# One layer of a streaming encoder with a mixture of experts: the last expert block's rows added into the results by transfers that add

## The chip, the cores and the metric

One Trainium2 chip, one of its cores. The metric is the device time of one execution in microseconds (us), the median of several runs. The core has TensorE (PE; PEld is its weight load), VectorE (DVE), ScalarE (ACT), GpSimd (POOL) and SyncE (SP), and 16 DMA engines that move data between HBM and on-chip memory. SP and ACT issue plain transfers on a queue of their own each (q1 and q10 in the profile); GpSimd issues indirect ones (q0), whose row addresses come from a list of indices.

## The reference, cut to what matters

544 tokens (32 of a running stream, 512 of a new one) of width 1024 pass through a mixer (attention and a gated delta net, summed into the residual x1) and then through a mixture of 32 experts. Each token has two experts, each with a weight:

```
h = silu(xb @ w_e1[e]) * (xb @ w_e3[e])          # w_e1, w_e3: 1024 x 512
yb = (h @ w_e2[e]) * weight                      # w_e2: 512 x 1024
y[token] += yb                                   # over the token's two choices
x2 = x1 + y                                      # the results y_prompt (512 rows) and y_sample (32 rows)
```

All data are fp32. Beside x2 the reference returns keys, values, forget logits and states, which the change does not touch.

## The kernel before

The program is a row of stages, each a `nc.Block()` with a written-out program for each engine; `k.run` ends a stage with a barrier of all engines (L130). The stages that matter here:

- **Projections** (`convolved_projections`, L508; its block is L542). TensorE multiplies the normalised tokens by 17 column chunks of the input projection. SP's program (L544 to L552) issues the loads of the weight chunks (through `Stream.load`, L425) and then two small stores, `logf_s` and `logf_p` (L550, L551). With these SP is done; the stage goes on until ScalarE has done its last SiLU (L540). The delta net stage follows (SP's first line in it is L837).
- **Routing** (`project_and_choose`, L2082; block L2103). It makes x1 rows in `k.x`, writes the normalised token rows into an HBM table, chooses two experts a token, and computes for each expert a list of up to 64 tokens (`k.idx`) and where each one's result goes (`k.dst`). It ends with three indirect gathers on GpSimd (L2140). Meanwhile SP fills the ring of weights, three slots of three matrices of 2 MB.
- **Experts** (`expert_blocks`, L2316; block L2468). One block of up to 64 tokens for each of 32 experts, in order 0 to 31, plus further blocks in a loop of `n` rounds where an expert has more than 64 tokens. In the profiled execution each of the block's instructions appears 32 times, so `n` is 0. All engines run the same order through `run_blocks` (L2440): six blocks written out, a loop over the middle, the rest written out, and the `n` further ones. Ahead of block 6 every engine waits for `planned`, the end of VectorE's arithmetic on the further blocks, which is spread over blocks 0 to 5 (`beside`, L2553).

For block b, in ring slot b % 3: TensorE transposes the gathered rows (L2385, L2387), multiplies by w1 and w3 (L2396), transposes the hidden values (L2401), multiplies by w2 (L2408). ScalarE does the SiLU (L2415) and copies the result to `y` (L2418). VectorE copies and multiplies (L2423, L2427, L2430). SP's `loads` (L2432) issues each weight matrix for block b as soon as block b - 3 has used the old one. GpSimd's `fetch` (L2360) gathers the rows for block b, and `scatter` (L2371) stores the result of block b: 128 half rows of 512 values, to the HBM table `choice_rows` (`k.ytok`, 4 x 544 half rows, one full row for each choice of each token). Every indirect transfer has a small copy or addition on GpSimd ahead of it (L2374, L2376).

The end: GpSimd waits until all blocks' rows are stored (L2514 to L2516) and signals `all_in` (L2517). SP and ACT then load the choice rows back (`load_rows`, L2461; SP the first choice of every token, ACT the second, five transfers each, in the order of the tiles: prompt 1 to 4, then sample). The rows land over the ring slot 0 of the weights (L2457), which block 30 used last. VectorE computes x = weight x row + x for five tiles and two choices (L2619), SP stores each tile to the result when both its sums are done (L2490) and waits for the five stores (L2491). Code with which the last part stands or falls:

```
for s in range(RING - 1):
    g.wait_ge(stored[s], 16 * len(range(s, NE, RING)))
g.wait_ge(stored[RING - 1], n * 16 + 16 * STEPS)
... .then_inc(all_in, 1)

eng.wait_ge(all_in, 1)                       # load_rows, on SP and ACT
for m, t in enumerate(ORDER): eng.dma_start(yrows[...], whole[...])
```

Of the kernel before, what the change touches and what calls it, by code (L numbers as in the profile page):

```python
# [18 lines left out]
ALU = mybir.AluOpType  # L19
# [3 lines left out]
D = 1024  # L23
# [120 lines left out]
def build(nc, ins, outs):  # L144
    k = Kernel(nc, ins, outs)
    k.chains = {}
    with k.top:
# [4 lines left out]
        k.got = [k.sem(f"y_got{m}", k.top) for m in range(10)]  # L152

        k.late = k.sem("late_stores", k.top)
        k.bank = [k.top.enter_context(nc.psum_tensor(f"bank{b}", [128, 512], F32)) for b in range(8)]
# [352 lines left out]
def convolved_projections(k):  # L508
# [6 lines left out]
    with ExitStack() as ctx:  # L515
# [9 lines left out]
        logged, rows, turned, copied = (k.sem("sm_" + n) for n in ("logged", "rows", "turned", "copied"))  # L525
        kept = k.sem("cv_kept")

        norms = Norms(k, "l2", [(k.cqk, c, DH ** -0.5 if c < 4 else 1.0, k.head_ones, 1.0,
# [13 lines left out]
        with nc.Block() as block:  # L542
            @block.sync
            def _(sp):  # L544
                for j in range(RAWS, NCC + 1):
                    s.load(sp, j)
                for j in range(RAWS):
                    s.load(sp, FOX0 + j)
                sp.wait_ge(copied, 1)
                sp.dma_start(k.o["logf_s"][0, 0], k.smt[0:NS, 0, 0:H]).then_inc(k.late, 16)  # L550
                sp.dma_start(k.o["logf_p"][0, 0].rearrange("(t p) h -> p t h", p=128), k.smt[:, 1:5, 0:H])\  # L551
                    .then_inc(k.late, 16)  # L552

            @block.gpsimd
# [1761 lines left out]
def expert_blocks(k):  # L2316

    nc = k.nc
    V = nc.vector
# [3 lines left out]
    with ExitStack() as ctx:  # L2326
        at = k.sb("b_index", [SLOTS, RING], I32, ctx)
        to = k.sb("b_target", [128, RING], I32, ctx)
        spare = k.sb("b_spare", [SLOTS, 4], F32, ctx)
        xg = k.xg  # L2330
# [11 lines left out]
        r1 = k.over("m_rank_oh", [128, 10, 2 * SLOTS], F32, "late", 12 * KD * FE + 4 * RING * D)  # L2342
        b1, cmpj, ejf = T("blk_oh", 10, MORE), T("cmpj", MORE, NE), T("ejf", MORE)
        names = ("index", "turned", "copied", "first", "up", "silu", "hidden", "hturned", "hcopied", "down", "out")
        index, turned, copied, first, up, silu, hidden, hturned, hcopied, down, out = (k.sem("b_" + n) for n in names)
        aimed, targets, diffs, exps, coded, listed, planned, all_in, added, summed = (k.sem("m_" + n) for n in (
            "aimed", "targets", "diffs", "exps", "coded", "listed", "planned", "all_in", "added", "summed"))
        gathered = k.gathered
# [22 lines left out]
        def scatter(g, b, slot):  # L2371

            g.wait_ge(out, b + 1)
            nc.gpsimd.tensor_copy(to[:, slot:slot + 1], k.dst[:, bass.ds(b, 1)]).then_inc(aimed, 1)  # L2374
            g.wait_ge(aimed, b + 1)
            nc.gpsimd.tensor_tensor(spare[:, 2:3], k.one[0:SLOTS, :], k.one[0:SLOTS, :], ALU.add)  # L2376
            g.indirect_dma_start(out=k.ytok, out_offset=bass.IndirectOffsetOnAxis(ap=to[:, slot:slot + 1], axis=0),  # L2377
                                 in_=y[:, slot, :], in_offset=None, bounds_check=4 * NT - 1, oob_is_err=False)\
                .then_inc(stored[slot], 16)

        def products(pe, b, slot, n, prev):
# [57 lines left out]

        def run_blocks(eng, part, beside=lambda s: None):  # L2440

# [26 lines left out]
        with nc.Block() as block:  # L2468
            @block.sync
            def _(sp):  # L2470
# [8 lines left out]
                for b in range(RING * STEPS, NE):  # L2479
                    loads(sp, b, b, b % RING, b - RING)  # L2480
                with sp.If(n > 0):
                    with sp.Fori(0, n) as j:
                        e = sp.value_load(k.eid[0:1, bass.ds(j, 1)], min_val=0, max_val=NE - 1)
                        loads(sp, e, j + NE, RING - 1, j + NE - 1)
                load_rows(sp, 0)
                for m, t in enumerate(ORDER):
# [3 lines left out]
                    sp.dma_start(dst, k.x[0:rows, t, :]).then_inc(summed, 16)  # L2490
                sp.wait_ge(summed, 80)  # L2491
                sp.wait_ge(k.late, 16 * 4)

            @block.gpsimd
            def _(g):
                g.wait_ge(targets, 1)
                for b in range(RING, EARLY + RING):
                    fetch(g, b, b % RING, b // RING, b - RING)
                    scatter(g, b - RING, b % RING)
                g.wait_ge(planned, 1)  # L2500
                n = g.value_load(k.nmore[0:1, 0:1], min_val=0, max_val=MORE)
                with g.Fori(EARLY // RING + 1, STEPS) as i:
                    for s in range(RING):
                        fetch(g, RING * i + s, s, i, RING * i + s - RING)
                        scatter(g, RING * i + s - RING, s)
                for b in range(RING * STEPS, NE + RING):
                    if b < NE:
                        fetch(g, b, b % RING, b // RING, b - RING)
                    scatter(g, b - RING, b % RING)
                with g.If(n > 0):  # L2510
                    with g.Fori(0, n) as j:
                        fetch(g, j + NE, RING - 1, j + STEPS, j + NE - 1)
                        scatter(g, j + NE, RING - 1)
                for s in range(RING - 1):  # L2514
                    g.wait_ge(stored[s], 16 * len(range(s, NE, RING)))
                g.wait_ge(stored[RING - 1], n * 16 + 16 * STEPS)  # L2516
                nc.gpsimd.tensor_tensor(spare[:, 3:4], k.one[0:SLOTS, :], k.one[0:SLOTS, :], ALU.add).then_inc(all_in, 1)  # L2517

            @block.tensor
            def _(pe):  # L2520
                def beside(b):
                    if b != 4:
                        return
                    pe.wait_ge(coded, 1)
                    for m in range(10):
                        j = m // 5
                        last = nc.tensor.matmul(M[:, MORE * j:MORE * j + MORE], r1[:, m, :], b1[:, m, :],  # L2527
                                                start=(m == 0), stop=(m == 9))
                    last.then_inc(listed, 1)
# [4 lines left out]
            def _(a):  # L2534
# [3 lines left out]
                run_blocks(a, scalar_part)  # L2538
                load_rows(a, 1)

            @block.vector
            def _(v):
# [10 lines left out]
                def beside(b):  # L2553
# [21 lines left out]
                    if b == 2:  # L2575
# [10 lines left out]
                        c(V.tensor_tensor(tv[:], more[:].rearrange("p (j t) -> p j t", j=2),  # L2586
                                          k.token[:].unsqueeze(1).broadcast_to([128, 2, 5]), ALU.mult))
                    if b == 3:
                        V.tensor_tensor(r1[:], k.iota[:].unsqueeze(1).broadcast_to([128, 10, 2 * SLOTS]),
                                        s_[:].unsqueeze(2).broadcast_to([128, 10, 2 * SLOTS]), ALU.is_equal)  # L2590
                        c(V.tensor_tensor(b1[:], k.iota[:, 0:MORE].unsqueeze(1).broadcast_to([128, 10, MORE]),
                                          blk[:].unsqueeze(2).broadcast_to([128, 10, MORE]), ALU.is_equal))
                        V.tensor_tensor(b1[:], b1[:], pairs(tv[:]).unsqueeze(2).broadcast_to([128, 10, MORE]), ALU.mult)\
                            .then_inc(coded, 1)
# [16 lines left out]
                aim(S, NE, k.dst[:, 0:NE]).then_inc(targets, 1)  # L2611
                run_blocks(v, vector_part, beside)
                for m, t in enumerate(ORDER):
                    rows = TILES[t][1]
                    for j in range(2):
                        v.wait_ge(k.got[2 * m + j], 16)
                        if j:
                            v.wait_ge(added, 2 * m + 1)
                        V.scalar_tensor_tensor(out=k.x[0:rows, t, :], in0=yrows[0:rows, t, j, :], scalar=k.wt[0:rows, t, j:j + 1],  # L2619
                                               in1=k.x[0:rows, t, :], op0=ALU.mult, op1=ALU.add).then_inc(added, 1)  # L2620

# [26 lines left out]
```

## Time and profile before

| | us |
|---|---|
| median of 3 runs (lowest, highest) | 1316.22 (1313.13, 1318.16) |
| the profiled execution's own time | 1313.6 |
| its span, first to last instruction | 1311.9 |
| PE busy | 1112.2 (85%) |
| DVE busy | 424.9 (32%) |
| ACT busy | 344.8 (26%) |
| POOL busy | 375.8 (29%) |
| mean of the granted TensorE clock | 0.935 of full speed |
| moved | 285.11 MB, mean 217 GB/s |

The profile is of one execution; times within it are microseconds from the span's start. A queue name such as SPq stands for what that engine's instruction queue did (issue of transfers, waits, drains). A DRAIN is the instruction with which an engine waits for its own work at the end of a stage. "Landing" is the moment at which a transfer raises its semaphore. In the chain that ended last, each piece is what released the next one.

### The profile page before, as it was taken

What the parts mean: (1) busy time and instruction counts of PE and PEld (TensorE: products, weight loads), DVE (VectorE), ACT (ScalarE), POOL (GpSimd) and SP (SyncE); (2) the same over time, 40 slices, a digit from 0 to 9 for tenths busy, and PEclk for the clock granted to TensorE, in tenths of its full rate; (3) what the DMA queues carried; (4) which work ended last, traced back from release to release, by engine and by line L of the source; (5) the groups of instructions that cost most, each with busy time, mean ns of one, the idle gap of its engine ahead of it and who ended that gap; (6) DMA issues with size and microseconds to landing.
All of it is one profiled execution on the core that took longest, in us unless ns stands there. A gap on an engine that the chain in (4) does not pass through costs nothing. (4 is left out here: it accounts for less than half of the span.)

```text
span 1311.9 us, 20441 instructions
## 1 busy us (share of the span) xinstructions
PE 1112.2 (85%) x8278; PEld 852.4 (65%) x8278; DVE 424.9 (32%) x921; ACT 344.8 (26%) x739; POOL 375.8 (29%) x410
## 2 busy tenths in 40 slices
PE   3999899889998959999899876888888878778881
PEld 2998898779998848888898654454444444444440
DVE  5497723881111354342323461311111000000004
ACT  5547623342222634443232311000000000000000
POOL 2354459621212452122454112112112111111100
PEclk9999989898989969999999877999999899998896
DMA  7222325244322511113421975999999999999975
GB/s 121 70 76 66 84 73 152 53 129 133 101 76 66 194 48 49 49 49 116 145 75 40 358 323 206 403 406 407 399 406 421 411 409 413 404 405 404 405 335 211
DMA packets 149146, 285.11 MB, mean 217 GB/s; under 512 B 43858, under 2 KB 119218, under 8 KB 132688
## 3 DMA queue, kind: packets, MB, share of 16 engines
q1 hardware_dynamic: 94112, 243.76, 49.3%
q10 hardware_dynamic: 49216, 29.17, 8.1%
q0 software_dynamic: 5744, 11.16, 2.5%
q8 instruction: 52, 0.85, 0.3%
q14 instruction: 22, 0.18, 0.0%
HBM read 267.60 MB, written 24.31 MB: 223 GB/s over the span
## 5 line engine op out<-in xcount | busy, mean ns | idle before, releaser
L450 POOL TENSOR_TENSOR cv_w_lo<-cv_w_raw,cv_w_hi 128x1024 fp32r<-128x1024 f32 (+1 forms) x69 | 161.9, 2346 | 385.4 <-ACT cv_w_hi L443 384.9
L464 PE MATMUL bank<-xhi,cv_w_hi 128*128 128x272 f32 x848 | 261.7, 309 | 10.5 <-POOL cv_w_lo L450 7.8
L2396 PE MATMUL bank<-e_w,b_xT 128*64 128x256 f32 x2048 | 233.0, 385 | 32.2 <-DVE b_xT L2423 24.5
L464 PE MATMUL bank<-xhi,cv_w_lo 128*128 128x272 f32 x848 | 251.9, 297 | 0.0
L464 PE MATMUL bank<-xlo,cv_w_hi 128*128 128x272 f32 x848 | 251.8, 297 | 0.0
L2396 PEld LDWEIGHTS bank<-e_w,b_xT 128*64 128x64 f32 x2048 | 145.4, 138 | 109.7 <-DVE b_xT L2423 29.8
L464 PEld LDWEIGHTS bank<-xhi,cv_w_hi 128*128 128x128 f32 x848 | 167.2, 197 | 15.6 <-POOL cv_w_lo L450 9.6
L464 PEld LDWEIGHTS bank<-xlo,cv_w_hi 128*128 128x128 f32 x848 | 167.7, 198 | 1.2
L464 PEld LDWEIGHTS bank<-xhi,cv_w_lo 128*128 128x128 f32 x848 | 167.0, 197 | 0.0
L2408 PE MATMUL bank<-e_w,b_hiddenT 128*64 128x512 f32 x512 | 130.0, 654 | 32.1 <-issue 18.4
L2374 POOL COPY b_target<-slot_target 128x1 int32 (+1 forms) x32 | 5.7, 178 | 370.2 <-ACT b_y L2418 370.2
L2408 PEld LDWEIGHTS bank<-e_w,b_hiddenT 128*64 128x64 f32 x512 | 40.6, 148 | 99.3 <-issue 79.9
L2418 ACT ACTIVATE b_y<-bank 128x512 f32<-128x512 f32 x32 | 19.1, 597 | 304.2 <-PE bank L2408 304.2
L2427 DVE TENSOR_TENSOR b_hidden<-b_silu,bank 128x256 f32<-128x256 f32 x32 | 13.5, 421 | 245.0 <-PE bank L2396 245.0
L443 ACT ACTIVATE cv_w_hi<-cv_w_raw 128x1024 fp32r<-128x1024 f32 (+1 forms) x69 | 69.3, 1004 | 29.1 <-DMA cv_w_raw<-in_w_br_a 17.5
L2423 DVE COPY b_xT<-bank 128x512 f32<-128x512 f32 x32 | 22.1, 692 | 160.1 <-PE bank L2387 160.1
L644 DVE SCALAR_TENSOR_TENSOR conv_acc<-conv_in,wconv,conv_acc 128x547 f32<-128x547 f32 x48 | 60.5, 1261 | 1.7
L2415 ACT ACTIVATE b_silu<-bank 128x256 f32<-128x256 f32 x32 | 12.3, 383 | 152.8 <-PE bank L2396 152.8
L1996 PE MATMUL bank<-o_hi,mix_prompt 128*128 128x512 f32 x128 | 44.2, 410 | 2.7 <-POOL o_lo L1989 1.9
L464 PE MATMUL bank<-yb_hi,cv_w_hi 128*128 128x272 f32 x128 | 39.8, 311 | 0.0
L2377 POOL DMA_INDIRECT choice_rows<-b_y,b_target x32 | 32.8, 1024 | 17.4 <-issue 17.4
L464 PE MATMUL bank<-yb_lo,cv_w_hi 128*128 128x272 f32 x128 | 37.4, 292 | 0.0
(430 smaller groups left out, 1641.9 us busy)
## 6 DMA issues: line engine op xcount, KB each, us to landing
e_w<-in_w_e SPq DMA_DIRECT2D x96, 2048.0 KB, 38.6
cv_w_raw<-in_w_in ACTq DMA_DIRECT2D x33, 512.0 KB, 4.2
cv_w_raw<-in_w_in SPq DMA_DIRECT2D x19, 512.0 KB, 3.9
cv_w_raw<-in_w_br_b ACTq DMA_DIRECT2D x8, 512.0 KB, 4.1
o_raw<-in_w_out SPq DMA_DIRECT2D x16, 256.0 KB, 4.5
g_values_gates<-g_z_stage ACTq DMA_DIRECT2D x12, 272.0 KB, 4.6
f_gates<-g_values_gates SPq DMA_DIRECT2D x2, 1088.0 KB, 8.7
x_in<-in_x_prompt SPq DMA_DIRECT2D x4, 512.0 KB, 7.1
```

Source lines behind the costliest of these rows:

```text
L443: self.k.nc.scalar.activation(self.whi[:, c % OPS, 0:nk, :], self.raw[:, c % RAWS, 0:nk, :], ACT.Copy)\
L450: self.k.nc.gpsimd.tensor_tensor(self.wlo[:, s, 0:nk, :], self.raw[:, s, 0:nk, :], self.whi[:, c % OPS, 0:nk, :].bitcast(F32), ALU.subtract)\
L464: last = self.k.nc.tensor.matmul(self.bank(c, h)[:, 0:HALF], w, x[:, d, cols], start=(d == 0 and n == 0), stop=(d == nk - 1 and n == 2))
L644: op = nc.vector.scalar_tensor_tensor(out=ac[:, 0:W], in0=ci[:, w:w + W], scalar=k.wconv[:, w, c:c + 1], in1=ac[:, 0:W], op0=ALU.mult, op1 ...
L1996: last = k.nc.tensor.matmul(bank[0:n, :], rows, w[:, d, :], start=(start and i == 0), stop=(d == KD - 1 and i == 2))
L2377: g.indirect_dma_start(out=k.ytok, out_offset=bass.IndirectOffsetOnAxis(ap=to[:, slot:slot + 1], axis=0), in_=y[:, slot, :], in_offset=Non ...
L2396: last = nc.tensor.matmul(k.bank[bank][sl[a], 0:FH], xT[:, d, :], w[slot][:, d, FH * a:FH * a + FH], start=(d == 0), stop=(d == KD - 1))
L2408: last = nc.tensor.matmul(k.bank[4][sl[a], :], hT[:, f % 2, sl[f // 2]], k.w2[slot][:, f, 512 * a:512 * a + 512], start=(f == 0), stop=(f ...
L2415: nc.scalar.activation(act[:], k.bank[1][:, 0:FH], ACT.Silu).then_inc(silu, 1)
L2418: nc.scalar.activation(y[:, slot, :], k.bank[4][:], ACT.Copy).then_inc(out, 1)
L2423: nc.vector.tensor_copy(xT[:].rearrange("p k s -> p (k s)"), k.bank[0][:]).then_inc(copied, 1)
L2427: nc.vector.tensor_tensor(hm[:], act[:], k.bank[2][:, 0:FH], ALU.mult).then_inc(hidden, 1)
```

## The change

- A new semaphore `blank`, and in the projection stage: VectorE zeroes a tile of 128 x 512 first, and SP, behind its two small stores, stores it 17 times over into the whole table `choice_rows` and waits for the landing. GpSimd waits for it again at the start of the expert stage.
- The expert stage's `all_in` is given once blocks 0 to 30 are stored. Block 31 is not stored to the table; its entries there stay zero. SP's `load_rows` comes before the loop of further blocks, ACT's between block 31's SiLU and its copy of y.
- VectorE sums the rows (`sum_rows`) after its part of block 31, then multiplies block 31's y by the slots' weights. GpSimd waits for the five result stores and then adds block 31's rows into y_s and y_p by two indirect transfers with `compute_op=ALU.add`. A list of indices leaves out rows that are not of that result. Further blocks, if any, are added in the same way, one by one.
- The plan arithmetic on VectorE and TensorE computes these weights and indices in addition.

```diff
 (convolved_projections, SP)
                 sp.dma_start(k.o["logf_p"][0, 0].rearrange("(t p) h -> p t h", p=128), k.smt[:, 1:5, 0:H])\
                     .then_inc(k.late, 16)
+                sp.wait_ge(blanked, 1)
+                sp.dma_start(k.ytok.rearrange("(p r) n -> p r n", p=128),
+                             blank[:].unsqueeze(1).broadcast_to([128, 4 * NT // 128, D // 2])).then_inc(k.blank, 16)
+                sp.wait_ge(k.blank, 16)
 (convolved_projections, DVE)
+                nc.vector.memset(blank[:], 0.0).then_inc(blanked, 1)
 (expert_blocks)
+        def add(g, slot, m, p_at, s_at, wait_between):
+            g.wait_ge(weighted, m + 1)
+            nc.gpsimd.tensor_tensor(spare[:, 3:4], k.one[0:SLOTS, :], k.one[0:SLOTS, :], ALU.add)
+            g.indirect_dma_start(out=k.o["y_s"][0].rearrange("t (two n) -> (t two) n", two=2),
+                                 out_offset=bass.IndirectOffsetOnAxis(ap=s_at, axis=0),
+                                 in_=y[:, slot, :], in_offset=None, bounds_check=2 * NS - 1, oob_is_err=False,
+                                 compute_op=ALU.add).then_inc(added_s, 16)
+            if wait_between:
+                ...
+            g.indirect_dma_start(out=k.o["y_p"][0].rearrange("t (two n) -> (t two) n", two=2),
+                                 out_offset=bass.IndirectOffsetOnAxis(ap=p_at, axis=0),
+                                 in_=y[:, slot, :], in_offset=None, bounds_check=2 * NP - 1, oob_is_err=False,
+                                 compute_op=ALU.add).then_inc(stored[slot], 16)
 (scalar_part)
             nc.scalar.activation(act[:], k.bank[1][:, 0:FH], ACT.Silu).then_inc(silu, 1)
+            if isinstance(b, int) and b == NE - 1:
+                load_rows(a, 1)
             a.wait_ge(down, b + 1)
 (run_blocks)
+            late(eng, NE - 1, (NE - 1) % RING, 0, wsl[:, 0:1])
             with eng.If(n > 0):
                 with eng.Fori(0, n) as j:
                     part(eng, j + NE, RING - 1, j + STEPS, j + NE - 1)
+                    late(eng, j + NE, RING - 1, j + 1, wcur[:])
 (GpSimd)
                 g.wait_ge(targets, 1)
+                g.wait_ge(k.blank, 16)
...
-                for b in range(RING * STEPS, NE + RING):
+                for b in range(RING * STEPS, NE + RING - 1):
                     if b < NE:
                         fetch(g, b, b % RING, b // RING, b - RING)
                     scatter(g, b - RING, b % RING)
+                for s in range(RING):
+                    g.wait_ge(stored[s], 16 * len(range(s, NE - 1, RING)))
+                nc.gpsimd.tensor_tensor(spare[:, 6:7], ..., ALU.add).then_inc(all_in, 1)
+                g.wait_ge(summed, 80)
+                last = (NE - 1) % RING
+                add(g, last, 0, at_p[:, 0:1], at_s[:, 0:1], False)
+                g.wait_ge(added_s, 16)
+                g.wait_ge(stored[last], 16 * len(range(last, NE, RING)))
 (DVE, plan arithmetic in block 5; two operations more each in blocks 2 and 3)
-                        aim(M, MORE, k.dst[:, NE:]).then_inc(planned, 1)
+                        c(V.tensor_copy(wsl[:], M[:, 2 * MORE:3 * MORE + 1]))
+                        for f, bank, one, two in ((slice(0, 1), S, NE - 1, 2 * NE - 1), (slice(1, MORE + 1), M, 0, MORE)):
+                            w = f.stop - f.start
+                            c(V.tensor_copy(fin[:, f], bank[:, one:one + w]))
+                            c(V.tensor_tensor(fin[:, f], fin[:, f], bank[:, two:two + w], ALU.add))
+                        ... five more on fin, far and at_p ...
+                        V.tensor_copy(at_s[:], fin[:]).then_inc(planned, 1)
 (PE, ten more small matmuls after block 4)
+                        last = nc.tensor.matmul(M[:, 2 * MORE:3 * MORE + 1], r1[:, m, :], bw[:, m, :], start=False, stop=(m == 9))
 (DVE, after block 31)
+                def weigh(v, b, slot, m, weight):
+                    if slot != RING - 1:
+                        sum_rows()
+                    else:
+                        v.wait_ge(aimed, 3 * m + NE - 1)
+                    v.wait_ge(out, b + 1)
+                    V.tensor_scalar(y[:, slot, :], y[:, slot, :], weight, None, ALU.mult).then_inc(weighted, 1)
```

## Rows read from the trace of the kernel before

**Rows 1.** Stretches: start:end us, PE PEld DVE ACT POOL busy, clock, DMA share, GB/s

```profile
830.00:900.00 70.00, 61.27 (x448) 33.91 (x445) 13.75 (x36) 4.33 (x10) 11.56 (x25) 0.98 1.01 404
1200.00:1270.00 70.00, 57.57 (x386) 30.21 (x384) 7.00 (x14) 3.92 (x8) 8.25 (x18) 0.93 1.00 405
```

**Rows 2.** Chain that ended last, 1286 to 1312: start us, us, what

```profile
1285.91 0.44 PE bank L2408 x2
...
1288.00 2.38 DMA choice_rows<-b_y,b_target
...
1290.82 0.33 SPq L2466
...
1291.19 7.34 DMA y_rows<-choice_rows
```

**Rows 3.** Timeline of the end: start us, us, engine line operation, idle before and releaser

```profile
1272.74 1.00 POOL L2377 DMA_INDIRECT choice_rows<-b_y,b_target  x1 [0.53 <-issue]
...
1287.30 0.18 POOL L2376 TENSOR_TENSOR b_spare<-one 64x1 f32<-64x1 f32 x1
1288.00 0.99 POOL L2377 DMA_INDIRECT choice_rows<-b_y,b_target  x1 [0.52 <-issue]
...
1295.83 13.13 DVE L2619 SCALAR_TENSOR_TENSOR x_rows<-y_rows,token_weight,x_rows 128x1024 f32<-128x1024 f32 x10 [13.46 <-DMA y_rows<-choice_rows]
...
1308.98 0.34 SPq L2490 DMA_DIRECT2D out_y_s<-x_rows  x1
```

**Rows 4.** DMA queues in 1278:1279 (two lines), 1279:1280, 1281:1282, 1282:1283: packets, MB, share

```profile
q1 hardware_dynamic: 5, 0.04, 9.7%
...
q0 software_dynamic: 4, 0.01, 2.1%
...
q1 hardware_dynamic: 7, 0.06, 13.5%
...
q1 hardware_dynamic: 3, 0.02, 5.8%
...
q1 hardware_dynamic: 1, 0.00, 0.1%
```

**Rows 5.** End of the projection stage: timeline, ScalarE's drain, DMA queue in 152:154

```profile
150.53 0.43 SPq L551 DMA_DIRECT2D out_logf_p<-small_rows  x1
...
159.95 1.33 SPq L837 DMA_DIRECT2D g_states<-in_state_gdn  x2
...
L542 ACTq DRAIN  x1: 776/776/776, 158.5 to 158.5; - x1
...
q1 hardware_dynamic: 996, 0.22, 50.7%
```

**Rows 6.** DMA queues over the span, and the last store's issue to landing

```profile
q1 hardware_dynamic: 94112, 243.76, 49.3%
q10 hardware_dynamic: 49216, 29.17, 8.1%
...
out_y_s<-x_rows SPq DMA_DIRECT2D x1, 128.0 KB, 1.9
```

**Rows 7.** GpSimd's drains (ns min/median/max, start), and the routing stage's last gather

```profile
L2468 POOLq DRAIN  x1: 5294/5294/5294, 1290.6 to 1290.6; - x1
...
L2103 POOLq DRAIN  x1: 4789/4789/4789, 790.1 to 790.1; - x1
...
791.62 0.95 POOL L2140 DMA_INDIRECT b_rows<-token_rows,slot_token  x1 [0.30 <-issue]
```

**Rows 8.** Timeline around the added small operations, and the plan's matmuls (ns)

```profile
36.37 0.56 DVE L620 TENSOR_SCALAR small_cols<-bank,sm_bias,sm_sign 96x272 f32<-96x272 f32 x1 [8.11 <-PE bank L464]
...
L2527 PE MATMUL bank<-m_blk_oh,m_rank_oh x20: 262/263/283, 867.8 to 869.9; 128*128 128x16 f32 x20
...
883.35 0.17 DVE L2551 CAST slot_target<-m_target 128x16 int32<-128x16 f32 x1
...
885.80 0.43 PE L2385 MATMUL bank<-ident,b_rows 64*128 64x64 f32 x2
```

More of the change, by code:

```diff
@@ L2438, in loads, with run_blocks @@
             load_down(k, sp, e, slot)
-        def run_blocks(eng, part, beside=lambda s: None):
+        def run_blocks(eng, part, beside=lambda s: None, late=lambda eng, b, slot, m, weight: None):
             for b in range(EARLY):
@@ L2491, in _ @@
                 sp.wait_ge(summed, 80)
+                with sp.If(n > 0):
+                    with sp.Fori(0, n) as j:
+                        e = sp.value_load(k.eid[0:1, bass.ds(j, 1)], min_val=0, max_val=NE - 1)
+                        loads(sp, e, j + NE, RING - 1, j + NE - 1)
                 sp.wait_ge(k.late, 16 * 4)
@@ L2512, in _ @@
                         fetch(g, j + NE, RING - 1, j + STEPS, j + NE - 1)
[L2513 to L2517, printed above, removed]
+                        for to_x, at_x in ((to_p, at_p), (to_s, at_s), (wcur, wsl)):
+                            nc.gpsimd.tensor_copy(to_x[:], at_x[:, bass.ds(j + 1, 1)]).then_inc(aimed, 1)
+                        g.wait_ge(aimed, 3 * j + NE + 2)
+                        nc.gpsimd.tensor_tensor(spare[:, 4:5], k.one[0:SLOTS, :], k.one[0:SLOTS, :], ALU.add)
+                        add(g, RING - 1, j + 1, to_p[:], to_s[:], True)
+                        g.wait_ge(stored[RING - 1], 16 * j + 16 * (STEPS + 1))
+                        nc.gpsimd.tensor_tensor(spare[:, 5:6], k.one[0:SLOTS, :], k.one[0:SLOTS, :], ALU.add)
             @block.tensor
@@ L2587, in beside @@
                                           k.token[:].unsqueeze(1).broadcast_to([128, 2, 5]), ALU.mult))
+                        wt = k.wt[:].rearrange("p t j -> p j t")
+                        c(V.tensor_tensor(wm[:], more[:].rearrange("p (j t) -> p j t", j=2), wt, ALU.mult))
+                        c(V.tensor_tensor(w0[:], wt, wm[:], ALU.subtract))
                     if b == 3:
@@ L2604, in beside, with sum_rows @@
                         c(V.tensor_tensor(k.idx[:, NE:], second[0:SLOTS, 0:MORE], M[0:SLOTS, MORE:2 * MORE], ALU.add))
-                        aim(M, MORE, k.dst[:, NE:]).then_inc(planned, 1)
+                        c(V.tensor_copy(wsl[:], M[:, 2 * MORE:3 * MORE + 1]))
[3 more added lines that the diff above has]
+                            c(V.tensor_tensor(fin[:, f], fin[:, f], bank[:, two:two + w], ALU.add))
+                        c(V.tensor_scalar(fin[:], fin[:], 2.0, half[:], ALU.mult, ALU.add))
+                        c(V.tensor_scalar(fin[:], fin[:], -2.0 * NT - 2.0 * NS, None, ALU.add))
+                        c(V.tensor_scalar(far[:], fin[:], 0.0, 4.0 * NT, ALU.is_lt, ALU.mult))
+                        c(V.tensor_tensor(far[:], far[:], fin[:], ALU.add))
+                        c(V.tensor_copy(at_p[:], far[:]))
+                        c(V.tensor_scalar(fin[:], fin[:], 2.0 * NS, None, ALU.add))
+                        V.tensor_copy(at_s[:], fin[:]).then_inc(planned, 1)
[6 more added lines that the diff above has]
+                    V.tensor_scalar(y[:, slot, :], y[:, slot, :], weight, None, ALU.mult).then_inc(weighted, 1)
+                def sum_rows():
+                    for m, t in enumerate(ORDER):
+                        rows = TILES[t][1]
+                        for j in range(2):
+                            v.wait_ge(k.got[2 * m + j], 16)
+                            if j:
+                                v.wait_ge(added, 2 * m + 1)
+                            V.scalar_tensor_tensor(out=k.x[0:rows, t, :], in0=yrows[0:rows, t, j, :],
+                                                   scalar=k.wt[0:rows, t, j:j + 1], in1=k.x[0:rows, t, :],
+                                                   op0=ALU.mult, op1=ALU.add).then_inc(added, 1)
                 c(V.memset(half[0:64, :], 4.0 * NT))
@@ L2611, in _ @@
                 aim(S, NE, k.dst[:, 0:NE]).then_inc(targets, 1)
[L2612 to L2620, printed above, removed]
+                run_blocks(v, vector_part, beside, weigh)
 _INS = ["x_prompt", "x_sample", "cache_fox_k", "cache_fox_v", "cache_fox_logf", "state_gdn", "state_gdn_conv", "g_mix",
```

25 lines of the change are left out of this document (15 added, 10 removed).

## The prediction

> **What bounds the kernel now.** I read four views. The stretches of the expert stage come first: the DMA engines are full, 404 and 405 GB/s, from its first weight loads nearly to its last [rows 1]. The stage is a stream of weights, and TensorE runs beside it; a microsecond won or lost on another engine inside the stream is worth nothing. The change leaves the bytes of that stream alone. So I look at what lies outside it.
>
> The chain that ended last shows the second part, after the last weights: block 31's rows go out (1288.00, landed after 2.38 us), then the row loads are issued (1290.82), the pair that starts the chain of sums lands 7.34 us into it, and only then is VectorE the limit [rows 2]. The timeline of the same stretch gives the durations: ten sums in 13.13 us from 1295.83, ended at 1308.96; the last store, y_s, issued at 1308.98 [rows 3]. It lands in 1.9 us [rows 6], so the results are all in memory at 1310.9, and the span ends 1.0 later, at 1311.9. Third, the end of the projection stage, where the change puts a store of 4.46 MB with a wait behind it [rows 5]. Fourth, what GpSimd's queue does after transfers of its own [rows 7].
>
> **The change, part by part.**
>
> *The clear, and SP's wait for it.* 4 x 544 rows of 2 KB are 4.46 MB. SP is free for it at 150.53 + 0.43 = 150.96 [rows 5]. A transfer's fixed part I take from y_s: 1.9 us for 128 KB, less the 0.3 that these bytes take at 405 GB/s, so 1.6 [rows 1, 6]. The bytes take 4.46 / 0.405 = 11.0 us. Small packets ahead of it in the same queue still keep the engines half busy between 152 and 154 [rows 5]: 0.5 us of that falls behind 152.6. Landing: 150.96 + 1.6 + 0.5 + 11.0 = 164.1. Today the last engine to reach the stage's end is ScalarE, whose drain ends at 158.5 + 0.78 = 159.3, and the next stage starts at 159.95 [rows 5]. SP's wait now holds this barrier, and all five engines stand behind it, TensorE too, with its next stage. Nothing later absorbs that, because the weight ring starts after it: **+4.8 us**. Bounds: nothing ahead in the queue gives 4.3; the rate of the ACT queue's rows, 29.17 MB in 8.1% of 16 engines' 1311.9 us, or 275 GB/s [rows 6], gives 16.2 us for the bytes and 10.0 for the delay. The zeroing of the source, one pass of 128 x 512 on VectorE, lies in its 8.11 us idle ahead of L620 [rows 8]; without that cover it costs under 1 us.
>
> *More plan arithmetic.* In block 5 VectorE gets 12 more small operations ahead of `planned`. The five there end at 883.35 + 0.17 = 883.5 and take 0.21 each, so the plan is ready at 886.0; TensorE starts block 6 at 885.80 [rows 8]: 0.2 us late. Ten more small matmuls after block 4 are as many as the 20 records of 263 ns there, under 2.7 us [rows 8]. The other extra operations (two in block 2, two in block 3) end before VectorE is next wanted. All of it delays TensorE under full DMA [rows 1], so **0**; were that cover gone, it would be up to 2.9 us. GpSimd's wait for the clear, 600 us old by then, is 0.
>
> *Rows loaded after block 30 in place of 31.* Block 30's indirect store is issued at 1272.74 [rows 3]. Its queue (q0) still has packets in 1278:1279 and none in 1279:1280 [rows 4]; I take 1278.9 as landed. From landing to the loads' issue it is 1290.82 - 1290.38 = 0.44 today [rows 2], so they go out at 1279.3, 11.5 us earlier. SP's queue has issued all its weights by then. But the last weights are not in: q1 moves packets until 1282.0, some 25 to 57 GB/s in all, that is on one or two DMA engines [rows 4]. Those engines are 2.7 us behind when the rows arrive, and a transfer lands with its slowest engine. So the pair that starts the chain of sums lands 2.7 later than its start allows: the gain is 11.5 - 2.7 = **-8.8 us**, and VectorE's sums end at 1300.2. Bounds: -11.5 (the tail disturbs nothing) and, with the tail counted twice, -6.1. ScalarE waits and issues five loads ahead of block 31's copy of y; block 31's down projection ends at 1286.35 [rows 2], or a few us later, well before its rows are wanted at 1302, so this is hidden. The copy would cost if `all_in` came after 1283.
>
> *The added rows.* From the stored results (VectorE's end + 1.9, as now) GpSimd has: wake 0.05, its small operation 0.18, gap 0.52 [rows 3], the indirect transfer to y_s 0.99 [rows 3], gap 0.30 before another [rows 7], the one to y_p, landed 2.38 after its start [rows 2]: 4.4. The multiply by the weight is ready long before. No row shows a transfer that adds. [...] **+5.0 us** (4.4 to 6.8).
>
> *The block's end.* This is the term without a clear row. GpSimd's drain at the end of this block lasted 5.29 us, although its last transfer had landed before it began and only an operation of 0.18 was left; it is hidden today, since it is over at 1295.9 and the span ends at 1311.9. At the end of the routing block a drain of 4.79 began while indirect transfers were still issuing, and ended 794.9 - 792.6 = 2.3 us behind the last of them (791.62 + 0.95) [rows 7]. After the change GpSimd is the last engine, and its drain comes after the landing. By the row nearest in form, the same drain in the same place, **+5.1 us**; the bounds are 0 (it was busy with the row loads' traffic) and 5.3.
>
> **Sum.** 4.8 - 8.8 + 5.0 + 5.1 = **+6.1 us**. The profiled execution took 1313.6 (span 1311.9 and 1.7 around it) and would take 1319.7; the median shown, 1316.22, lies 2.6 above it, and I predict against the median: 1322.3. Half a per cent, 6.6 us, is about what a measurement of this kernel can tell from no change; the sum lies just inside.
>
> **The rivals.**
>
> *The drain is short.* For it: the routing block's, 0.4 us or less behind its landing; against: the one in this very place. Sum 4.8 - 8.8 + 5.0 = +1.0: 1317.2. Chance 0.25.
>
> *The weights' tail is shared.* ACT's row loads go to the same slow DMA engines as SP's last weights. If the engines serve both in turn, 2.7 us of tail takes 5.4 and the sums start that much later: -6.1, sum +8.8: 1325.0. For it: 1 or 2 engines carry the whole tail [rows 4]. Against: the pair that decides may be on ACT's queue, which has no tail of its own. [...] Chance 0.12.
>
> *Slower: the clear is slow.* One mechanism, at the barrier at 159.3: the clear goes at 275 GB/s and lands at 169.3. It adds 5.2 to the sum, +11.3: 1327.5. It decides from a landing at 164.7 on, if the rest is as forecast, and from 169.7 with a short drain. For it: ACT's average [rows 6]; against: 405 with large rows [rows 1]. Chance 0.13.
>
> *Faster side.* Everything at its lower bound: clear 4.3, rows -11.5, added rows 4.4, no drain: -2.8, 1313.4. Chance 0.10.
>
> *The change does not do what it says.* The clear's wait does not hold the barrier (SP's part ends elsewhere than I read), and the drain is short: 1.0 - 4.8 = -3.8, 1312.4. Chance 0.03.
>
> **How the numbers follow.** The forecast keeps 0.37. Around it the terms spread by some 2 us and the bound of 6.6 cuts it: 0.17 slower, 0.20 same. The short drain and the faster side lie within half a per cent save for the spread and some luck of the layout, 0.07 of it faster. The two slow rivals are slower but for 0.05. That makes faster 0.09, same 0.53, slower 0.38. The range goes from the faster rival's 1313.4, rounded down, to the slow clear's 1327.5: 1313 to 1328; it leaves out ends of both kinds.
>
> **What would show it.** Right: the start of the delta stage at 164 to 165 in place of 159.95; row loads issued near 1279.3 plus that shift; VectorE's sums ending 8.8 earlier against it; an indirect pair behind the last store, landed 5 us on; a drain of GpSimd at the very end of about 5 us. Wrong: a stage start unmoved; sums that begin late because the tail of the weights grew; a drain under 1 us; or a slower weight stream, which would say that the cover I named was not there.

## The result, and the profile after

Measured in turns with the kernel before: 1321.81 us (1319.26 to 1326.18) against 1313.13 (1308.94 to 1320.61), ratio 1.0066 with a 95% interval of 1.0041 to 1.0091. That is 8.7 us slower, from 5.4 to 11.9. I had put 1322.3, in a range from 1313 to 1328, and a sum of +6.1. The profiled execution took 1326.18, the longest of its seven, with a span of 1324.5; so terms are read inside it, between neighbouring events, and not from the two spans.

**The end of the projection stage** (timeline, with the store's time to landing), against [rows 5]:

```profile
150.10 0.43 SPq L553 DMA_DIRECT2D out_logf_p<-small_rows  x1
150.57 0.62 SPq L556 DMA_DIRECT2D choice_rows<-cv_blank  x1
158.11 0.61 ACT L542 ACTIVATE conv_v<-conv_acc 128x512 f32<-128x512 f32 x1
165.35 1.32 SPq L844 DMA_DIRECT2D g_states<-in_state_gdn  x2
...
DMA to landing us min/median/max: 13.9/13.9/13.9
```

The clear is one transfer of 4352 KB, issued at 150.57 and landed at 164.5; ScalarE's last SiLU ends at 158.7. The next stage starts at 165.35, where it was 159.95, although this execution was 0.43 ahead at the small stores (150.10 against 150.53). Here and below a stage's length is taken from one closing barrier to the next, by the start of GpSimd's drain there (L130): the projection stage has 138.6 us, where it had 133.0.

**What moved while it waited** (DMA in 40 slices of the stretch 150 to 166, so 0.4 us each):

```profile
DMA  4889999999999999999999999999999997100000
GB/s 52 138 228 346 347 268 303 333 404 410 410 410 410 404 404 410 410 404 410 410 410 410 404 410 410 404 410 410 410 404 399 404 399 266 51 5 0 0 0 0
```

From the ninth slice, 153.2, to 163.2 the clear has the engines nearly to itself, at 399 to 410 GB/s; then the rate falls off over three slices (266, 51, 5). Its rows of 2 KB moved as fast as the weight stream does, whose stretches have 404 and 405 GB/s.

**The end** (timeline), against [rows 3]:

```profile
1282.63 1.00 POOL L2390 DMA_INDIRECT choice_rows<-b_y,b_target  x1 [0.52 <-issue]
1289.44 2.82 SPq L2500 DMA_DIRECT2D y_rows<-choice_rows  x5
1294.54 5.27 DVE L2683 SCALAR_TENSOR_TENSOR x_rows<-y_rows,token_weight,x_rows 128x1024 f32<-128x1024 f32 x4 [2.27 <-DMA y_rows<-choice_rows]
1296.29 0.60 ACT L2449 ACTIVATE b_y<-bank 128x512 f32<-128x512 f32 x1 [9.63 <-PE bank L2437]
1300.73 2.67 DVE L2683 SCALAR_TENSOR_TENSOR x_rows<-y_rows,token_weight,x_rows 128x1024 f32<-128x1024 f32 x2 [0.92 <-DMA y_rows<-choice_rows]
1304.53 5.23 DVE L2683 SCALAR_TENSOR_TENSOR x_rows<-y_rows,token_weight,x_rows 128x1024 f32<-128x1024 f32 x4 [1.13 <-DMA y_rows<-choice_rows]
1309.79 0.33 SPq L2520 DMA_DIRECT2D out_y_s<-x_rows  x1
1311.82 0.19 POOL L2397 TENSOR_TENSOR b_spare<-one 64x1 f32<-64x1 f32 x1 [22.41 <-DMA out_y_s<-x_rows]
1312.60 1.62 POOL L2398 DMA_INDIRECT out_y_s<-b_y,m_at_s  x1 [0.59 <-issue]
1314.53 1.58 POOL L2405 DMA_INDIRECT out_y_p<-b_y,m_at_p  x1 [0.31 <-issue]
```

Take block 30's store as the zero of both profiles. Before, the sums ended 1308.96 - 1272.74 = 36.2 us behind its issue; now it is 1309.76 - 1282.63 = 27.1: the rows part gave **9.1 us**. The loads go out 6.8 us behind block 30's store, where it was 18.1, so 11.3 earlier; from their issue to the sums' end it is 20.3 us, where it was 18.1, so 2.2 more. The sums begin as soon behind the loads as before (5.1 us against 5.0), and the first four run back to back; the other six wait twice for rows (0.92, 1.13).

Then the tail that the change adds. From the sums' end to the span's end it was 1311.9 - 1308.96 = 2.9 us; it is 1324.5 - 1309.76 = 14.7. The last transfer's landing and GpSimd's drain fill it (landing of L2405; drains of the block, ns and start), against [rows 7]:

```profile
DMA to landing us min/median/max: 3.7/3.7/3.7
...
L2502 POOLq DRAIN  x1: 5129/5129/5129, 1318.5 to 1318.5; - x1
L2502 SPq DRAIN  x1: 13/13/13, 1312.1 to 1312.1; - x1
```

SP is at its drain at 1312.1, all other engines earlier. The last landing is at 1314.53 + 3.7 = 1318.2; the drain begins at 1318.5 and lasts 5.13.

**The plan arithmetic** (VectorE and TensorE around block 5's end), against [rows 8]:

```profile
894.36 3.65 PE L2437 MATMUL bank<-e_w,b_hiddenT 128*64 128x512 f32 x16 [0.52 <-DVE b_hiddenT L2461]
...
896.95 0.18 DVE L2665 CAST m_at_s<-m_final 128x17 int32<-128x17 f32 x1
```

The plan is ready at 897.1, and TensorE is busy with block 5 until 898.0, so it does not wait for the plan.

### The profile page after: what moved, and what is told of

Same layout as the page of the kernel before. It is cut to its first block and busy times, and to the rows that moved or that the text cites. A ratio compares the mean times of both kernels' runs of the same rounds, so it can differ in the third digit from the quotient of the medians.

```text
span 1324.5 us, 20497 instructions
## 1 busy us (share of the span) xinstructions
PE 1113.7 (84%) x8298; PEld 853.5 (64%) x8298; DVE 431.1 (33%) x934; ACT 345.1 (26%) x739; POOL 377.9 (29%) x410
## 5 line engine op out<-in xcount | busy, mean ns | idle before, releaser
L2458 DVE TENSOR_TENSOR b_hidden<-b_silu,bank 128x256 f32<-128x256 f32 x32 | 13.5, 422 | 248.7 <-PE bank L2425 248.7
L465 PE MATMUL bank<-yb_hi,cv_w_lo 128*128 128x272 f32 x128 | 37.3, 291 | 0.0
## 6 DMA issues: line engine op xcount, KB each, us to landing
choice_rows<-cv_blank SPq DMA_DIRECT2D x1, 4352.0 KB, 13.9
```

What stands on the lines that cost most here:

```text
L465: last = self.k.nc.tensor.matmul(self.bank(c, h)[:, 0:HALF], w, x[:, d, cols], start=(d == 0 and n == 0), stop=(d == nk - 1 and n == 2))
L2458: nc.vector.tensor_tensor(hm[:], act[:], k.bank[2][:, 0:FH], ALU.mult).then_inc(hidden, 1)
```

## The experiments

All are edits of the changed kernel unless said otherwise. The profiles of several executions showed one thing to allow for first. The delta net stage, which no edit touches, has anything from 258.0 to 266.2 us in them (264.2 before, 265.3 in the changed kernel, 258.9 in the first experiment, 258.5 in the third), and the expert stage also varies by a few us. So each run's own term is read in its profile, and the medians are used for the total only. Each median and ratio is against the kernel before, on the same chip. The changed kernel itself was timed again only beside the last version, so where a total is compared with its ratio of 1.0066, the two come from different chips, and each has an uncertainty of some 3 us.

The end of the kernel can be read more sharply. From the end of VectorE's sums to the end of the span it is 2.9 us in the kernel before and 14.7 in every execution with the adds and the block's drain unchanged (14.69 to 14.75 in four profiles). The experiments below move this figure.

### The clear alone, on the kernel before

```diff
 (kernel before; the clear, its zeroed tile and both waits as in the change, nothing else)
+                sp.wait_ge(blanked, 1)
+                sp.dma_start(k.ytok.rearrange("(p r) n -> p r n", p=128), blank[:].unsqueeze(1)...).then_inc(k.blank, 16)
+                sp.wait_ge(k.blank, 16)
```

> The kernel before plus the clear of the choice table and SP's wait for it, nothing else (the table is later filled as before). Theory (the wait holds the stage's barrier until the clear has landed, and nothing later absorbs it): the delta net stage starts 5.0 to 6.0 us after its place before (about 165 in place of 159.95), and the time is 5 to 6 us above the kernel before. Rival (the clear is hidden by later slack, or its only cost is in the stage): stage start moved, but the total within 2 us of before.

Measured: 1320.28 against 1314.67 us, ratio 1.0059 (1.0034 to 1.0083), so 4.5 to 10.9 us. In its profile the projection stage lasts from 27.1 to 165.8, 138.7 us, where it was 133.0 before and 138.6 in the changed kernel. The theory holds: **5.7 us** at the barrier (5.6 in the changed kernel), and the total has them too. (In the nine profiles with the clear at this place the stage has 138.2 to 138.7 us in seven and 136.6 and 136.8 in two; without it there, 132.6 to 133.3.) The clear alone costs most of what the whole change does; by their own terms the other parts add up to +2.5 us, which the two totals cannot tell from nothing.

### The clear in 17 pieces

```diff
-                for j in range(RAWS, NCC + 1):
-                    s.load(sp, j)
-                for j in range(RAWS):
-                    s.load(sp, FOX0 + j)
+                rows17 = k.ytok.rearrange("(p r) n -> p r n", p=128)
+                for r, j in enumerate(list(range(RAWS, NCC + 1)) + [FOX0 + j for j in range(RAWS)]):
+                    s.load(sp, j)
+                    if r == 0:
+                        sp.wait_ge(blanked, 1)
+                    sp.dma_start(rows17[:, r, :], blank[:]).then_inc(k.blank, 16)
... (behind the two small stores, the one large store and its wait are left out)
+                sp.wait_ge(k.blank, 16 * 17)
```

> The changed kernel with the clear cut into 17 stores of 256 KB, one behind each weight load of the projection stage, and SP's wait at the same place. Theory (the clear costs only because it stands at the end of the stage, 5.9 us there): the delta net stage starts within 1 us of its place in the kernel before, and the time is 4.5 to 6 us below the changed kernel, so 2 to 4 us above the kernel before. Rival (bytes of the clear cost wherever they move, by delaying the weight loads): the stage start stays at 163 or later, the time as the changed kernel's.

Measured: 1312.69 against 1314.67, ratio 1.0003 (0.9975 to 1.003). The stage lasts 133.2 us, as before the change (133.0). The same bytes, spread behind weight loads, cost nothing there: from 27 to 150 us the DMA engines are busy for a share of 0.29 in the kernel before and of 0.42 here. The price was that of the place. The total is lower than I expected (level with before, where I had 2 to 4 above), but its interval, from 3.3 below to 3.9 above, takes that in.

### One more drain, where GpSimd waits anyway

```diff
                 nc.gpsimd.tensor_tensor(spare[:, 6:7], ..., ALU.add).then_inc(all_in, 1)
+                g.drain()
```

> The changed kernel with one more drain on GpSimd, right behind its signal that blocks 0 to 30 are stored, where it waits some 20 us for the sums anyway. Theory A (the drain's 5.1 us is work on the transfers GpSimd has issued since its last drain, 60 of them): the early drain takes about 5 us, hidden, and the last one, with two transfers behind it, under 1.5 us; the time falls by 3.5 to 5 us against the changed kernel. Theory B (the price is fixed for any drain that has indirect transfers behind it): the last drain stays at 4.5 to 5.3 us and the time stays.

The two drains in its profile, the added one (L2548) and the block's:

```profile
L2548 POOLq DRAIN  x1: 5221/5221/5221, 1281.2 to 1281.2; - x1
...
L2502 POOLq DRAIN  x1: 219/219/219, 1310.8 to 1310.8; - x1
```

Measured: 1315.02 against 1314.67, ratio 1.0014 (0.9988 to 1.004), against the changed kernel's 1.0066; from the sums' end to the span's end it is 9.8 us in place of 14.7. Theory A holds: the early drain takes the 5.2 us, under the row loads and sums, and the last one, with two transfers behind it, 0.22. That it lasts about as long in the middle of the row loads as the last one does with the DMA engines idle also says that their traffic has little part in it, 0.26 us at most (5.22 here against 4.96 for as many transfers in the run without adds, below).

### The block ended without GpSimd's drain

```diff
-        with nc.Block() as block:
+        with nc.Block(no_gpsimd_drain=True) as block:
```

> The changed kernel with the last block ended by semaphores only, GpSimd's own drain left out there (it has waited for the landing of each of its transfers). The program's closing barrier still has a drain of 0.03 us in its place. Theory A (a backlog has to be worked off by whichever drain comes first): the 5.1 us move to the closing barrier's drain and the time stays as the changed kernel's. Rival (the cost belongs to that one drain's form): it vanishes, the time falls by 5 us.

Measured: 1317.21 against 1314.67, ratio 1.0031 (1.0 to 1.0061). Here theory A's detail failed and the rival was right: the drains of the closing barriers stay at 0.03 to 0.05 us, and at L2502, where GpSimd's drain had 5.13, its queue has none.

```profile
1309.42 1.58 POOL L2405 DMA_INDIRECT out_y_p<-b_y,m_at_p  x1 [0.30 <-issue]
...
L130 POOLq DRAIN  x8: 34/36/47, 25.7 to 1313.9; - x8
```

The last landing is at 1309.42 + 3.7 = 1313.1 and the span ends at 1314.2, 1.1 later, where it was 6.3 later in the changed kernel; from the sums' end to the span's end it is 9.5 us in place of 14.7. So the 5.1 us belong to the block's own drain, and no later drain takes them over. GpSimd has waited for the landing of each of its transfers here, so the results do not depend on that drain.

### A drain in the middle: by number, or fixed

```diff
+                g.drain()
                 for b in range(RING * STEPS, NE + RING - 1):
```

> The changed kernel with one more drain on GpSimd behind its loop over the middle blocks, so that the last drain has 6 block transfers and the 2 that add behind it in place of 62. Theory A1 (the price goes by the number of transfers since the last drain, 5.1 us for some 60): the drain in the middle takes about 4.5 us and the last one 0.2 to 1.2 us. Theory A2 (a fixed price as soon as a few block transfers lie behind it): the last one takes 4.5 to 5.3 us.

The block's drain in its profile:

```profile
L2502 POOLq DRAIN  x1: 709/709/709, 1319.4 to 1319.4; - x1
```

(The one time it was run gave 1322.62 us; the middle drain took 10.6 us, so "about 4.5" missed: it began at 1219.9, as block 26's store was being issued, and ended at 1230.5, 2.3 behind that store's landing at 1228.2 in full traffic.) The last drain took 0.71 us with 8 transfers behind it. With the others that began when GpSimd had nothing running this makes a line:

| indirect transfers since the last drain | drain, us | run |
|---|---|---|
| 2 | 0.219 | drain early |
| 8 | 0.709 | drain in the middle |
| 60 | 4.963 | no adds, below |
| 62 | 5.129 | the changed kernel |

From the first two, (0.709 - 0.219) / 6 = 0.082 us a transfer and 0.055 fixed; for 60 and 62 this gives 4.96 and 5.12. The price goes by the number of transfers. It does not go by their indices (128 for a block's store and for an add, 64 for a gather): a line through the first two rows by indices would give 4.5 us for the third. Two more drains lie 0.26 us above the line, the early one (60 transfers, 5.22) and the one of the kernel before (61, 5.29). Both began while the small addition of 0.18 us was still running on GpSimd. A drain does wait for such work: in the projection stage of the kernel before, with no indirect transfer behind it, one of 3.05 us spans an operation of 2.95.

### The end without the adds

```diff
-                add(g, last, 0, at_p[:, 0:1], at_s[:, 0:1], False)
-                g.wait_ge(added_s, 16)
-                g.wait_ge(stored[last], 16 * len(range(last, NE, RING)))
```

Block 31's rows are left out of the results.

> The changed kernel without the two transfers that add: block 31's rows are left out of the results. Theory (adds and drain stand alone at the end, behind SP's wait for the stores): the program's span ends about 1 us behind the landing of y_s, if GpSimd's drain, which now starts when its last wait for the sums is over, still takes 5 us, then 5 us behind that; so either 6.4 us (adds alone) less than the changed kernel, or, were the drain free when nothing was just issued, 11.5 us less. By the drain_early run I expect the first: a backlog of 60 transfers is worked off at 5.1 us wherever the drain stands.

```profile
1300.36 0.33 SPq L2520 DMA_DIRECT2D out_y_s<-x_rows  x1
...
L2502 POOLq DRAIN  x1: 4963/4963/4963, 1302.5 to 1302.5; - x1
```

Measured: 1315.14 against 1312.41, ratio 1.0029 (1.0004 to 1.0054). The first case: the drain starts once GpSimd's wait for the sums is over, 1302.5, and the span ends at 1308.3, 8.0 us behind the sums' end in place of 14.7, so 6.7 less. The drain became visible because GpSimd waits for the end, not because of the adds.

### Plain stores in place of adds

```diff
-                                 compute_op=ALU.add).then_inc(added_s, 16)
+                                 ).then_inc(added_s, 16)
 (and the same for y_p)
```

Block 31's rows overwrite the sums of their tokens.

> The changed kernel with its two last transfers as plain indirect stores (block 31's rows overwrite the sums in place of being added to them). Theory (adding costs GpSimd 0.6 us more for each transfer and 1.3 us more to landing): each transfer takes 1.0 us on GpSimd in place of 1.6, the second lands 2.4 us after its start in place of 3.7, and the way from the sums' store to the landing is 3.0 to 3.7 us in place of 6.4... the sum of both differences being 2 to 2.7 us. Rival (the price is in the 128 indices with most of them out of range, not in the adding): durations stay at 1.6 and 3.7.

Once, 1318.83 us. Its timeline, and the landing of the last one, which is the first figure:

```profile
1306.51 0.19 POOL L2397 TENSOR_TENSOR b_spare<-one 64x1 f32<-64x1 f32 x1 [22.44 <-DMA out_y_s<-x_rows]
1307.28 0.98 POOL L2398 DMA_INDIRECT out_y_s<-b_y,m_at_s  x1 [0.58 <-issue]
1308.57 0.98 POOL L2404 DMA_INDIRECT out_y_p<-b_y,m_at_p  x1 [0.30 <-issue]
...
DMA to landing us min/median/max: 2.3/5.9/8.2
```

(2.3 is the indirect one; the others are the tiles' stores.) The way from 1306.51 to the landing at 1310.9 is 4.4 us, against 6.4 from 1311.82 to 1318.2 with adds: adding costs **2.0 us**, 0.6 on GpSimd for each transfer and 0.8 in flight behind the second. The rival falls: the lists of indices are the same, and without the adding the durations are back at 1.0 and 2.3. The difference is as expected; the 3.0 to 3.7 that I gave for the whole way was too low.

### Row loads held until the weights' tail is in

```diff
+                g.wait_ge(k.w2_loaded[(NE - 1) % RING], 16 * len(range((NE - 1) % RING, NE, RING)))
                 nc.gpsimd.tensor_tensor(spare[:, 6:7], ..., ALU.add).then_inc(all_in, 1)
```

> The changed kernel, where GpSimd waits for block 31's last weights to land before it lets the row loads go. Theory (the sums are held up by the DMA engines that still carry the weights' tail, so an issue before the tail's end gains nothing): the loads go out 1.5 to 3.5 us later measured from block 30's store, but VectorE's sums end within 1 us of where they do in the changed kernel, 27.1 us behind the issue of block 30's store, and last 18 to 19 us from issue to end in place of 20.3. Rival (the loads' spread is their own): the sums end later by the whole delay.

Once, 1322.82 us. From its timeline:

```profile
1277.45 1.00 POOL L2390 DMA_INDIRECT choice_rows<-b_y,b_target  x1 [0.53 <-issue]
1287.46 0.18 POOL L2548 TENSOR_TENSOR b_spare<-one 64x1 f32<-64x1 f32 x1 [9.01 <-DMA e_w<-in_w_e]
1287.67 3.45 SPq L2500 DMA_DIRECT2D y_rows<-choice_rows  x5
1292.87 7.86 DVE L2684 SCALAR_TENSOR_TENSOR x_rows<-y_rows,token_weight,x_rows 128x1024 f32<-128x1024 f32 x6 [5.79 <-DMA y_rows<-choice_rows]
1300.98 5.23 DVE L2684 SCALAR_TENSOR_TENSOR x_rows<-y_rows,token_weight,x_rows 128x1024 f32<-128x1024 f32 x4 [0.26 <-DMA y_rows<-choice_rows]
```

The loads go out 10.2 us behind block 30's store in place of 6.8, so 3.4 later; the sums end 28.8 behind it in place of 27.1, so 1.6 later. Neither theory is quite right. The time from issue to sums' end falls back to 18.5 us, nearly the 18.1 of before, so the tail does cost 1.8 of the 20.3 (the ten profiles with the loads let go at once have 20.0 to 21.3). That 1.6 of the 3.4 us are still won by starting into it is less sure: of those ten, nine end their sums 26.8 to 27.4 us behind the store and one, the clear in 17 pieces, 28.2, and this was one execution.

### A version that beats both

```diff
 (the clear in 17 pieces, as above, and)
-    with nc.Block() as block:                          # routing
+    with nc.Block(no_gpsimd_drain=True) as block:
-        with nc.Block() as block:                      # experts
+        with nc.Block(no_gpsimd_drain=True) as block:
```

> The changed kernel with the clear in 17 pieces behind the weight loads, and with the routing and the expert block ended without GpSimd's drain. Theory (from the runs so far: clear 5.3 us, last drain 5.1 us; in the routing stage the drain holds the barrier for 2.3 us behind its last instruction): 12 to 13 us below the changed kernel, so 3 to 5 us below the kernel before, ratio 0.996 to 0.998. Rival (the routing drain's time is the landing of its gathers, which the next stage then waits for): 10 to 11 below the changed kernel, within 2.5 us of before.

Measured: 1304.98 against 1312.41, ratio 0.9934 (0.9902 to 0.9966), better than the 0.996 to 0.998 expected. Run again on another chip, beside the changed kernel:

> The changed kernel once more, beside the next one on the same chip. Theory (clear 5.5, rows -9.1, adds 6.4, drain 5.1, and 0.3 between): ratio to the kernel before 1.004 to 1.008, and in its profile 14 to 15.5 us from the end of VectorE's sums to the end of the span (2.9 before).

> The version with the clear in 17 pieces and two blocks ended without GpSimd's drain, once more. Theory: 12 to 14 us below the changed kernel on the same chip, ratio to the kernel before 0.993 to 0.998.

The changed kernel had 1322.68 against 1313.26, ratio 1.006 (1.0034 to 1.0087), with 1315.0 - 1300.3 = 14.7 us from the sums' end to the span's; this version 1306.77, ratio 0.9957 (0.993 to 0.9984), 15.9 below it by the medians, where I had 12 to 14. The terms read in the profiles (5.6 for the clear, 5.2 at the end, 2.5 in the routing stage) add up to 13.3; the rest is within what the medians leave open. It beats the kernel before twice, by 2.1 us at the least by the second interval. In its routing stage the last gather and two of the next stage's first instructions, and behind them TensorE's first one in the kernel before:

```profile
790.67 0.94 POOL L2146 DMA_INDIRECT b_rows<-token_rows,slot_token  x1 [0.30 <-issue]
...
792.27 0.66 PE L2413 MATMUL bank<-ident,b_rows 64*128 64x64 f32 x2 [5.60 <-PEq L130]
792.30 0.06 DVE L2686 MEMSET m_half<- 64x1 f32 x1 [5.10 <-PEq L130]
...
795.75 0.66 PE L2385 MATMUL bank<-ident,b_rows 64*128 64x64 f32 x2 [8.14 <-PEq L130]
```

From the gather's end, 791.6, it is 0.7 us to TensorE's start; before it was 795.8 - 792.6 = 3.2. So that drain, too, held a barrier, for 2.5 us. Most of it was a wait for gathers that no one needed yet: in this version the three land at 791.0, 793.2 and 793.7, and TensorE begins on the first one's rows at 792.3.

## Why the prediction was right

By its own steps, with what was measured in the changed kernel:

| step | predicted | measured | from |
|---|---|---|---|
| clear and SP's wait | +4.8 | +5.6 | stage 138.6 against 133.0; alone 138.7 |
| plan arithmetic | 0 | 0 | ready 0.9 us ahead of TensorE |
| rows behind block 30 | -8.8 | -9.1 | 36.2 to 27.1 behind block 30's store |
| added rows | +5.0 | +6.5 | y_s landed (1311.7) to last landing (1318.2) |
| the block's drain | +5.1 | +5.1 | 5.129 |
| sum | +6.1 | +8.1 | median moved by +8.7 (5.4 to 11.9) |

**The clear.** Its place, the barrier that it holds and that nothing later gives the time back were right, each shown by an experiment. It was 0.8 short, nearly all of it in the landing, which took 13.9 us from the issue where I had 13.1 (13.5 to 13.9 in the nine profiles). The rate in between was right (399 to 410 GB/s, where I had 405), and so was the start: the rate is full from 153.2, where I had 153.1. What I left out lies at the end: the rate falls off from 163.2 until the last row is through at 164.1, and the landing follows 0.35 later.

**The rows.** Block 30's store landed 6.5 us behind its issue (1289.15), where I had read 6.2 from the packets of its queue. The last weights landed 3.1 us behind the loads' issue, and this tail cost 1.8 to 2.2 us where I had 2.7. Its place was wrong in my account: I let the pair of rows that starts the sums land late, but the sums began 5.1 us behind the loads, as before, and it is the later rows that came late. My reading of the chain had the same slip, without effect on the sum: 7.34 us is the landing of the second tile's first row (1291.19 + 7.34 = 1298.53), while the sums had begun at 1295.83. That a transfer lands with its slowest engine can be read in this trace: block 30's store raised its semaphore in 16 steps, 12 of them by 1285.3 and the last at 1289.15. The rival that the tail is shared out and costs 5.4 did not come: the tail slowed the row loads by less than its own length of 3.1. No run shows how the packets of the queues alternated on an engine.

**The added rows.** This term was the one most off, by 1.5 us. I took the GpSimd time of an indirect transfer, 0.99, from the plain ones; with adding it is 1.62 and 1.58. And 3.7 us to landing is 1.3 above the plain 2.38, where I had allowed 0.6. No run shows that 0.6, which was my estimate; what plain stores in the same place show is 0.6 less on GpSimd for each transfer and 0.8 less in flight behind the second. The sum of both, 6.5, lies inside the bound that I gave, 6.8.

**The drain.** The choice between two rows was right, for a reason that I did not have, so this term was in part luck. I took the row nearest in form; in truth the two drains differed by the number of indirect transfers behind them, 61 against 3 (and five plain ones of GpSimd, whose price no run shows apart). By the line above, 3 cost 0.3 us; the routing drain ended 0.4 behind the landing of its last gather.

The case "slower by over 0.5%" had 0.38 and "same" 0.53. The measured ratio, 1.0066, lies just past the line that the sum lay just short of, because the clear and the adds were short by 2.3 us together; its interval, 1.0041 to 1.0091, takes in both sides of the line. That the time itself, 1321.81, came within 0.5 us of my 1322.3 is luck: the kernel before had 1313.13 beside it and not 1316.22, and the change was 2.6 us larger than my sum. The slow clear at 275 GB/s and the clear that holds no barrier are both refuted by the profile.

## What to carry to other kernels

A transfer that is only "early" is not free: look at what its wait stands in front of, and cut it into pieces behind loads that leave the DMA engines idle (here 5.7 us for one piece at the stage's end and 0.2 for 17 pieces, which took the engines' busy share from 0.29 to 0.42). When the last wait of a stage moves to GpSimd, its drain moves to the critical path, at 0.08 us for each indirect transfer since the last drain in these runs; drain once earlier, where it waits anyway, or leave the drain out when each transfer has been waited for, since no later drain took its time over here. A change that trades the end of one chain for another should be costed event by event from a common zero, since the terms (9 us won, 12 us lost at the end) are larger than their sum.

## What the runs showed of the hardware that I had not expected

- GpSimd's drain at a block's end costs 0.055 us, and 0.082 more for each indirect transfer since the last drain: 0.22, 0.71, 4.96 and 5.13 us for 2, 8, 60 and 62, with all of them landed before it began. The drain in the closing barrier took 0.05 us with the same 62 behind it; why it escapes stays open.
- An indirect transfer that adds costs GpSimd 1.6 us in place of 1.0, and 3.7 us to landing in place of 2.3.
- The delta net stage has a different length in each execution, with the same instructions: 258.0 to 266.2 us in the thirteen profiles, not at two levels but with values in between (261.2, 261.5, 262.8). Two of them, with the columns of [rows 1]:

```profile
159.95:424.00 264.05, 250.99 (x2181) 227.85 (x2181) 91.64 (x176) 82.83 (x170) 106.98 (x111) 0.90 0.37 99
...
166.00:424.70 258.70, 248.70 (x2181) 225.69 (x2181) 91.01 (x176) 82.84 (x170) 107.22 (x111) 0.91 0.37 101
```

  The first is the kernel before, the second the clear alone. The granted clock differs by 0.01 on average (over all thirteen it goes from 0.90 to 0.93, the highest in the shortest); what decides the length was not tried. The spread is as large as the change's whole effect, so the times of single executions could not have told the two kernels apart.
